# A blockwise triangular inverse whose small matmuls stream 32 of 64 columns

## The reference, cut to what matters

```
def step(state, inp):
    r_t, w_t, k_t, v_t, kk_t, a_t = inp
    sa = jnp.einsum('bhij,bhj->bhi', state, -kk_t)
    state = (state * w_t[:, :, None, :] + sa[..., None] * (kk_t * a_t)[:, :, None, :]
             + v_t[..., None] * k_t[:, :, None, :])
    return state, jnp.einsum('bhij,bhj->bhi', state, r_t)
...
y = direction(0, False) + direction(1, True)
```

## Time and profile before

| | us |
|---|---|
| median of 3 runs | 4278.34 |
| lowest, highest | 4276.24, 4279.28 |
| the profiled execution | 4285.27 |
| its span, first to last instruction | 4283.4 |
| PE busy in the span | 4141.5 (97%) |
| PEld busy | 2695.0 (63%) |
| DVE busy | 1414.3 (33%) |
| mean granted TensorE clock | 0.992 of 2.4 GHz |

### The profile page before, as it was taken

The page is one execution under the profiler, slowest core; times in us unless marked ns, Lnnn a source line. Parts: engine busy times, 40 slices in busy tenths (PEclk is TensorE's granted clock), DMA queues, the critical chain, the costliest instruction groups (busy, mean ns, idle before and its releaser), DMA issues.

```text
span 4283.4 us, 60619 instructions
## 1 busy us (share of the span) xinstructions
PE 4141.5 (97%) x25176; PEld 2695.0 (63%) x25176; DVE 1414.3 (33%) x3578; ACT 868.6 (20%) x2216; POOL 324.8 (8%) x274
## 2 busy tenths in 40 slices
PE   8999999999999999999999999899999999999999
PEld 4666664444444666674434444687887788788878
DVE  4666631121002666650121000432234431323342
ACT  4232320010001233320010000332322212223220
POOL 0122300000000023210000000000110000011000
PEclk9999999999999999999999999999999999999999
DMA  3011112212221111002222222111111121111111
GB/s 121 33 37 35 45 41 88 80 63 79 74 79 64 50 45 45 31 22 94 85 69 72 76 78 74 54 55 55 59 55 53 57 69 60 50 60 60 57 58 64
DMA packets 71487, 261.60 MB, mean 61 GB/s; under 512 B 7936, under 2 KB 8064, under 8 KB 70960
## 3 DMA queue, kind: packets, MB, share of 16 engines
q1 hardware_dynamic: 69312, 250.62, 16.8%
q10 hardware_dynamic: 1904, 7.11, 0.5%
HBM read 253.51 MB, written 4.19 MB: 60 GB/s over the span
## 4 chain that ended last, share of the span: by engine, by line
PE 94%; DVE 3%; issue 1%; ACT 1%; DVEq 1%; ACTq 0%; DMA 0%; SPq 0%
PE ps L2238 30%; PE ps L1422 26%; PE ps L2372 10%; PE ps L2337 4%; PE ps L1441 2%; PE ps L1525 2%; PE ps L815 2%; PE ps L1585 2%; PE ps L773 2%; PE ps L2249 1%; PE ps L1544 1%; PE ps L2259 1%; PE ps L805 1%; PE ps L2280 1%; PE ps L858 1%
## 5 line engine op out<-in xcount | busy, mean ns | idle before, releaser
L2238 PE MATMUL ps<-xT,ring 128*128 128x512 f32 x2656 | 1163.4, 598 | 23.6 <-ACT xT L2428 23.6
L2238 PEld LDWEIGHTS ps<-xT,ring 128*128 128x128 f32 x2656 | 505.8, 192 | 657.9 <-issue 653.8
L1422 PE MATMUL ps<-xT,ring 128*128 128x264 f32 (+2 forms) x3392 | 782.7, 386 | 0.0
L1422 PEld LDWEIGHTS ps<-xT,ring 128*128 128x128 f32 (+1 forms) x3392 | 633.7, 190 | 110.3 <-issue 10.8
L2372 PE MATMUL ps<-arena,ring 128*128 128x512 f32 x1024 | 440.4, 593 | 1.9 <-issue 1.9
L2372 PEld LDWEIGHTS ps<-arena,ring 128*128 128x128 f32 x1024 | 194.5, 190 | 247.9 <-issue 247.9
L1422 PE MATMUL ps<-arena,ring 128*128 128x264 f32 (+1 forms) x1408 | 321.8, 386 | 5.9 <-DVE arena L1902 3.6
L1422 PEld LDWEIGHTS ps<-arena,ring 128*128 128x128 f32 x1408 | 266.7, 191 | 50.9 <-DVE arena L1902 5.1
L1672 ACT ACTIVATE arena<-ps 128x264 f32<-128x264 f32 (+8 forms) x316 | 122.3, 388 | 619.2 <-PE ps L1422 544.0
L2625 DVE TENSOR_TENSOR arena<-arena 128x512 f32<-128x512 f32 x64 | 44.3, 692 | 394.6 <-ACT arena L2491 394.6
L2337 PE MATMUL ps<-yT,ring 128*128 128x512 f32 x384 | 167.6, 593 | 2.3 <-ACT yT L1039 2.3
(11 more groups left out here) (334 smaller groups left out, 4599.8 us busy)
## 6 DMA issues: line engine op xcount, KB each, us to landing
ring<-in_weights SPq DMA_DIRECT2D x467, 512.0 KB, 3.4
arena<-skew_dram ACTq DMA_DIRECT2D x8, 448.0 KB, 3.0
arena<-in_x SPq DMA_DIRECT2D x1, 2048.0 KB, 7.6
out_rows<-arena SPq DMA_DIRECT2D x8, 256.0 KB, 2.9
skew_dram<-arena ACTq DMA_DIRECT2D x4, 511.5 KB, 5.8
consts<-in_const SPq DMA_DIRECT2D x1, 1256.0 KB, 10.2
consts<-in_const ACTq DMA_DIRECT2D x1, 1252.0 KB, 5.5
consts<-in_const SPq DMA_DIRECT2D x1, 128.0 KB, 2.3
```

The costliest lines, as they stand in the source:

```text
L1422: mm = pe.matmul(o[0:m, 0:cols.stop - cols.start], ws[:, k, 0:m], src[:, k, cols], start=k == 0, stop=k == nk - 1)
L2238: m = pe.matmul(o, w[:, k, :], src[:, k, 0:S], start=k == 0, stop=k == KD - 1)
```

## The change

The functions `level_w`, `level_x` and `level_t` give the matmul a moving operand and an output that hold only the changed blocks: with `blocks(z, e, b)`, 64 columns are seen as pairs of blocks of b columns, and block e of each pair is taken. That leaves 32 columns in 32/b pieces of b columns (16 pieces of 2 at level 2, one piece of 32 at level 32). The weights keep their 64 columns. Two products keep all 64 moving columns at one level, because DVE reads them all there: `level_w` at b = 2 and `level_t` at b = 32. The number and the order of instructions are the same on every engine.

```diff
+            def blocks(z, e, b):
+
+                return z.rearrange("p (x e b) -> p x e b", e=2, b=b)[:, :, e, :]
+
             def level_w(d, b, x):
...
                     r = half[e]
-                    m = pe.matmul(o[e][half[e ^ h], k], g1[d][h][r, n, 0, r], X[d][e ^ h][r, n, :], start=True, stop=True)
+                    w, x_ = o[e][half[e ^ h], k], X[d][e ^ h][r, n, :]
+                    if b > LEVELS[0]:
+                        w, x_ = blocks(w, d, b), blocks(x_, d, b)
+                    m = pe.matmul(w, g1[d][h][r, n, 0, r], x_, start=True, stop=True)
                 v.close_two(m)
...
                     f = half[e ^ h]
-                    m = pe.matmul(o[e ^ h][half[e], k], XT[d][h][f, n, :], W[d][e][f, n, :], start=True, stop=True)
+                    m = pe.matmul(blocks(o[e ^ h][half[e], k], d, b), XT[d][h][f, n, :], blocks(W[d][e][f, n, :], d, b),
+                                  start=True, stop=True)
                 v.close_two(m)
...
                             f = half[e ^ h]
-                            m = pe.matmul(o[h][f, HB * n:HB * n + HB], W[d][e][f, n, :], XT[d][h][f, n, :], start=True, stop=True)
+                            t, xt = o[h][f, HB * n:HB * n + HB], XT[d][h][f, n, :]
+                            if b < LEVELS[-1]:
+                                t, xt = blocks(t, 1 - d, b), blocks(xt, 1 - d, b)
+                            m = pe.matmul(t, W[d][e][f, n, :], xt, start=True, stop=True)
```

## The result

| | before | changed |
|---|---|---|
| median of 13 runs each, us | 4279.78 | 4291.86 |
| lowest, highest, us | 4274.24, 4291.74 | 4284.23, 4303.52 |
| ratio, 95% interval | | 1.0029, 1.002 to 1.0038 |
| profiled execution: time, span, us | 4285.27, 4283.4 | 4302.61, 4300.8 |
| mean granted TensorE clock there | 0.992 | 0.982 |

The changed kernel loses about 12 us. Its time lies inside the range of the prediction, but it is not "no change": it moved by more than its interval and by more than the 0.2% named there, upwards. The execution that was profiled is one of the three slowest of the 13, so its trace shows more of the loss than a typical run has.

What follows compares the result with a forecast made beforehand. PE, busy 97% of the span, was taken to bound the kernel. 4285.27 - 0 - 1.3 + 0 gave 4284.0 us for the profiled execution, or 4277.0 as a median (4278.34 - 1.3); range 4264 to 4300.

Steps and rivals of the forecast that it cites:

- The sum: Profiled execution 4285.27 us, less 0 for pace, less 1.3 for earlier hand-overs, plus 0 for access in pieces: 4284.0 us.
- rival 3: In the levels the clock falls to half; 6 us in each group costs 21 us, up to 125 throughout; chance 9%.
- "issue" pieces: Stretches where PE waits for nothing the profile shows; 34 with 20.0 us before X, which might absorb gains.
- The forecast of no change: Whole kernel: load sets the pace, pieces are free, clock stays; 77%, own range 4270 to 4284 us.
- the small form of the rival: One 6 us spell of half clock in each of eight groups, costing 21 us, 4298 us.
- The pace term: 6656 narrowed passes of W, X and T save 0 each, since the weight load keeps the slot at 56 to 60 ns.
- Rival 1: Moving columns set the pace of W, X and T passes; 35 to 60 us faster, about 4230 us; chance 7%.
- Pieces: Moving operand and output in pieces of 2 to 32 columns with gaps, taken to cost 0.
- the bound of 7 us: Most that access in pieces could cost W, X and T passes, from DVE's 1.8 ns a column.
- rival 2: Access in pieces slows PE's passes: +109 us at four times the column price, 19 us if only two-column pieces suffer; 7%.
- The tail: Last pass before a hand-over to DVE ends 28 ns earlier; 1.3 us saved, bounds 0 and 2.7.
- The count of 46: Waits where the path returns through DVE, 27 of W and 19 of X; times 28 ns gives 1.3 us.

Runs made afterwards that it cites:

- e9: The kernel before, with the moving operand narrowed to 32 columns only at levels 8, 16 and 32; ratio 1.0021.
- e3: The changed kernel with masks zero and W and T streaming only the first 16 columns in one piece, X as in the change; ratio 1.0132.
- e2: The changed kernel with masks zero and W and T streaming the first 32 columns in one piece, X still in pieces; ratio 1.0035.
- e1b: The changed kernel run and profiled once more, against the kernel before; 4297.42 us against 4282.45, ratio 1.0043.
- e1: The kernel before with all 64 columns kept, but read and written in the same pieces as in the change; 4280.94 us against 4282.45, ratio 0.9999.
- e7: The changed kernel with masks zero and W and T loading 32 weight columns and streaming 32 moving columns; 4282.59 us, ratio 1.0004 to the kernel before.
- e8: W and T load 32 weight columns but stream 64, masks zero, X as in the change; ratio 0.9998 to the kernel before.
- e4: Only the T product narrowed to 32 columns, W and X as in the kernel before; ratio 1.0.
- e11: The kernel before with all 64 columns, its T product going round four quarters instead of two at level 32 alone; ratio 1.0.

## Why the prediction was right and wrong

**The step that failed is the one that lets the clock stay at 1.00 in the levels.** The sum, 4285.27 - 0 - 1.3 + 0, has no term for it; the only cover was that the matmuls follow each other at the same pace. The runs showed 96 and 68 us of low clock in the eight stretches of the changed kernel, where there had been none, and 12 us lost in the median in place of 1.3 gained. The same event stood beside the sum as rival 3, named with its place and its mechanism and given 9%. Three things went wrong in it:

- The argument against it, that the matmuls follow each other at the same pace and in the same number, holds and doesn't help. With 987 matmuls and PE busy 28.09 of 32.6 us the clock fell all the same. In the profile busy time is the time in which some matmul is under way, and a 32-column pass counts like a 64-column one. The row that should have warned was the earlier trace rows: there the clock fell behind 65 matmuls with 5.29 of 7 us busy, and although PE had gaps there, they are no longer than about 1 us. So a steady stream of matmuls was no proven cover.
- The price. The prediction put 6 us of low clock in each group at 21 us, 0.44 us lost for each us of low clock, as if all of a spell were paced by PE. In the table the change lost 23.4 for 96 (0.24), e9 13.6 for 55 (0.25), e3 53.3 for 216 (0.25), e2 15.6 for 71 (0.22) and e1b 11.4 for 68 (0.17). By the 4 us of e1 each of these losses is uncertain by about 4 us, so e3 gives the firmest price. The factor for a pass was near (30 T passes 1.09 and 1.79 us, 1.64 against the 1.81 of the prediction). But only a part of a stretch is paced by PE. DVE is busy for 168 us at either clock, and PE's "issue" pieces, for the matmuls alone, shrank from 16.3 to 9.3 us in the changed kernel: what PE lost to the clock came in part out of its idle time. The prediction had this at hand, since by its own figures passes fill 154 of the 248.6 us, and 0.44 x 154 / 248.6 is 0.27. The amount was nearer. The two traces have 96 and 68 us against its 48; for a typical run it can be estimated from the mean clock of the span, 0.986 in the median of the 13 runs and 0.993 in that of the executions of the kernel before recorded beside the other runs, which makes 2 x 0.007 x 4290 = 60 us. So the rival gave a loss of 21 us where 12 were measured: its mechanism was right, and its price nearly twice too high.
- The chance. The forecast of no change had 77% although no row showed a stretch with so few columns streamed at full clock. That was an extrapolation, as the pieces were. The range reached up to 4300 for the small form of the rival, and that 4291.86 lies in it is owed to this bound and not to the forecast, whose own range ended at 4284.

**The pace term was right.** 6656 x 0: e1, e3, e7 and e8 show that a quarter's slot is the longer of load and stream, 56 to 60 ns for either at 64 columns, and that narrowing the moving side alone leaves it. The prediction read this from L957 beside L858, outside the levels, and that carried over. Rival 1 is out.

**Pieces were free**, as taken (e1); the bound of 7 us and rival 2 were not needed. The row of DVE that the bound came from said nothing of PE, so that they are free was a good guess until e1.

**The tail** of 28 ns is there in part. The shortest matmul of the T line fell from 213 to 186 ns, by 27. From the start of a T run to DVE's first op on it, level 4, before 145.61 - 144.41 = 1.20 us and after 145.10 - 143.92 = 1.18:

```profile
145.61 0.61 DVE L1321 SCALAR_TENSOR_TENSOR arena<-ps,lam,arena 128x128 f32<-128x128 f32 x2 [0.27 <-PE ps L815]
```

```profile
145.10 0.61 DVE L1332 SCALAR_TENSOR_TENSOR arena<-ps,lam,arena 128x128 f32<-128x128 f32 x2 [0.24 <-PE ps L826]
```

About 20 ns a hand-over, at this one and at the next. At full clock 46 of them would be worth 1 us. The count of 46 is a little high: the 19 waits of X are 14 of its loads and 5 of its matmuls, and the two can be the same hand-over. Either way it can't be told from noise: e4, which has it for T alone and keeps its clock, measures 1.0 and its stretches 249.3 us, as before.

**The "issue" pieces** were rightly seen as something that takes back what PE gains; e11 shows it, 5.0 us less PE work and 6.3 us more of these pieces. Their size was misread. The 34 pieces with 20.0 us of the earlier trace rows are those of loads and matmuls together; the matmuls alone have 10 with 7.7 us. The forecast does not hang on it.

## What to carry to other kernels

Before narrowing a matmul's moving operand, compare it with its weight load: on one part of the array the longer of the two is the price, so streaming fewer columns than there are weight columns saves nothing but the tail. Then look at the clock as well as the busy share, since a stretch in which PE stays busy with small passes can lose its clock when they get smaller. Price a spell of low clock by the part of the stretch that PE paces, and not by the whole. If the parts of a change cost nothing one at a time and the whole does, look for such a switch and not for a price per instruction.

## What the runs showed of the hardware

- The granted clock fell to 1.2 GHz in stretches with PE busy for some 28 of 32 us, at an unchanged cadence of matmuls and loads, once 32 in place of 64 columns were streamed in all three products (68 and 96 us of low clock in two executions, none before); with 16 columns in two of three products it was low for 216 of 302.6 us. The same program had the low spells in other stretches from one execution to the next.
- Four 64x64 quarters of the array run side by side, and each has its own slot: 15 ns a pass in four quarters, 30 in two, for the same operands (T 0.69 and 1.1 us for 32 passes).
- A moving operand and a PSUM output in pieces of 2 to 16 float32 columns are read and written at the pace of a whole one (e1 against before at full clock, X and T: 0.70 and 1.09 us in both at level 2, 0.63 for 30 passes and 1.15 for 32 in both at level 16).
- One us at half clock cost 0.17 to 0.25 us of these stretches (0.25 in e3, the firmest), not 0.5, since other things than PE pace much of them.
- Where the load of 64 weight columns paces a quarter, 64, 32 or 16 moving columns leave 32 loads in two quarters at 1.01 us; with 32 weight and 32 moving columns they take 0.58 us, and with 32 weight and 64 moving columns 0.92.
